# Expert 3's first late gate page: from two row blocks over all 128 partitions to two halves of 64 partitions, asked for at one release

## The reference

```python
def expert_block(args):
    xb, e = args
    hb = jax.nn.silu(xb @ w_gate[e]) * (xb @ w_up[e])
    return hb @ w_down[e]
```

## Time and profile before

| | us |
|---|---|
| median of 3 runs | 1267.19 |
| lowest and highest | 1266.06, 1267.52 |
| the profiled execution | 1266.4 |
| its span | 1264.6 |
| PE busy in the span | 1043.2 (82%) |
| DVE busy | 478.1 (38%) |
| ACT busy | 234.7 (19%) |

### The profile page before, as it was taken

How to read it: one execution, slowest core, us unless ns; L and a number is a source line. 1 busy time by engine, 2 the same in 40 slices (tenths; PEclk the granted TensorE clock), 3 DMA queues, 4 the chain that set the end, 5 groups by cost and what they waited for, 6 DMA issues and landing times.

```text
span 1264.6 us, 22376 instructions
## 1 busy us (share of the span) xinstructions
PE 1043.2 (82%) x9529; PEld 712.1 (56%) x9529; DVE 478.1 (38%) x1230; ACT 234.7 (19%) x526; POOL 4.9 (0%) x27
## 2 busy tenths in 40 slices
PE   9999998766766575889999999999977665758576
PEld 7888755434334352548888888876543333425243
DVE  2342543532222222237665556464343222222223
ACT  2221121111111111113433334121111111111111
POOL 1000000000000000000000000000000000000000
PEclk9999998978787887899999999999887878878789
DMA  9888799999999999996676664899999999999997
GB/s 341 238 338 336 249 430 426 426 428 430 428 429 427 429 429 429 428 392 191 191 230 228 225 217 150 338 362 429 425 428 428 429 427 430 428 430 427 429 428 294
DMA packets 98305, 461.49 MB, mean 365 GB/s; under 512 B 17468, under 2 KB 60728, under 8 KB 73400
## 3 DMA queue, kind: packets, MB, share of 16 engines
q1 hardware_dynamic: 97872, 460.34, 90.6%
q10 hardware_dynamic: 360, 0.15, 0.0%
HBM read 459.38 MB, written 1.08 MB: 364 GB/s over the span
## 4 chain that ended last, share of the span: by engine, by line
PE 52%; DMA 44%; ACT 1%; DVE 1%; issue 1%; SPq 1%; POOL 0%; POOLq 0%; DVEq 0%; ACTq 0%
DMA front<-in_expert_w_up 38%; PE pa L1535 10%; PE pa L1829 8%; PE pb L1535 8%; DMA arena<-in_expert_w_down 6%; PE wa L1829 5%; PE acc L1566 4%; PE wb L1859 3%; PE acc L1684 2%; PE pb L1609 1%; PE acc L1869 1%; PE pb L1785 1%; ACT arena L607 1%; PE wa L2124 1%; DMA w_x<-in_odd_out_proj 1%
## 5 line engine op out<-in xcount | busy, mean ns | idle before, releaser
L1829 PE MATMUL pa<-front,arena 128*32 128x256 f32 x1792 | 127.6, 448 | 77.0 <-DMA front<-in_expert_w_up 77.0
L1290 DVE TENSOR_SCALAR lower<-lower 128x128 f32<-128x128 f32 x64 | 14.4, 225 | 419.1 <-ACT lower L607 419.1
L1829 PE MATMUL wa<-front,arena 128*32 128x256 f32 x1232 | 98.0, 484 | 87.5 <-DMA front<-in_expert_w_up 84.0
L1829 PEld LDWEIGHTS pa<-front,arena 128*32 128x32 f32 x1792 | 62.9, 128 | 144.1 <-DMA front<-in_expert_w_up 89.8
L1829 PEld LDWEIGHTS wa<-front,arena 128*32 128x32 f32 x1232 | 46.9, 138 | 141.6 <-DMA front<-in_expert_w_up 94.0
L607 ACT ACTIVATE arena<-wb 32x256 f32<-32x256 f32 (+2 forms) x236 | 88.9, 377 | 103.4 <-PE wb L1859 95.1
L1859 PE MATMUL wb<-w_dn,conv_raw 128*32 128x256 f32 x1472 | 87.9, 379 | 1.0 <-DMA w_dn<-in_expert_w_down 1.0
L1829 PE MATMUL wa<-w_x,arena 128*32 128x256 f32 x896 | 68.3, 470 | 21.5 <-DMA w_x<-in_expert_w_up 21.5
L1535 PE MATMUL pa<-hnT,w_x 128*128 128x256 f32 x384 | 85.1, 380 | 0.0
L1535 PEld LDWEIGHTS pa<-hnT,w_x 128*128 128x128 f32 x384 | 72.5, 190 | 10.0 <-issue 0.3
L1535 PE MATMUL pb<-hnT,w_x 128*128 128x256 f32 x336 | 74.5, 380 | 0.0
(11 more groups left out here) (345 smaller groups left out, 1248.3 us busy)
## 6 DMA issues: line engine op xcount, KB each, us to landing
w_dn<-in_expert_w_down SPq DMA_DIRECT2D x46, 2048.0 KB, 26.4
front<-in_expert_w_gate SPq DMA_DIRECT2D x42, 2048.0 KB, 20.6
front<-in_expert_w_up SPq DMA_DIRECT2D x42, 2048.0 KB, 25.1
w_x<-in_expert_w_gate SPq DMA_DIRECT2D x15, 2048.0 KB, 31.4
w_x<-in_expert_w_up SPq DMA_DIRECT2D x15, 2048.0 KB, 35.8
arena<-in_expert_w_down SPq DMA_DIRECT2D x14, 2048.0 KB, 25.9
w_x<-in_odd_in_proj SPq DMA_DIRECT2D x16, 1024.0 KB, 5.5
front<-in_expert_w_up SPq DMA_DIRECT2D x10, 1024.0 KB, 8.9
```

The source lines that it names most:

```text
L1290: link(v.tensor_scalar(eg, eg, 1.0, None, ALU.add))
L1829: ins = mm(gu[32 * j:32 * j + 32, :, :], xb[:, k, c0:c0 + CAP], w[k][:, :, P * j:P * j + P], start=(k == 0), stop=(k == KC - 1))
```

## The change

One loop in `expert_stream` is rewritten. It runs once per layer. The bytes, their source, their place in `front` and the increments of the semaphore are the same; the cut and the time of the first request are not.

```diff
                 quarter(l, 3, 0, 0, "gu_res")
+                sp_.wait_ge(S["gu_half"], RELEASES * l + 2)
+                w = expert_w_gate[l, 3].rearrange("(p k) f -> p k f", k=KC)
                 for n in range(2):
-                    sp_.wait_ge(S["gu_half"], RELEASES * l + n + 1)
-                    quarter(l, 3, 0, 1, "gu_in0", 2 * n, 2 * n + 2)
+                    rows = slice(64 * n, 64 * n + 64)
+                    sp_.dma_start(late3[rows, 1, 0], w[rows, 4:8, :]).then_inc(S["gu_in0"], 16)
                 sp_.wait_ge(S["gu_half"], RELEASES * l + 3)
                 quarter(l, 3, 1, 1, "gu_in0")
```

## The result

| | before | after |
|---|---|---|
| median of 22 runs, us | 1266.59 | 1268.32 |
| lowest and highest | 1265.69, 1267.60 | 1267.69, 1269.04 |
| span of the profiled execution | 1264.6 | 1266.5 |

The ratio is 1.0014, with a 95% interval of 1.0008 to 1.0019: 1.7 us slower, about 0.9 us per layer. The forecast was 1.5 us slower.

What follows compares the result with a forecast made beforehand. PE was taken to set the pace early in each MoE stage, then the DMA queue; 16x - 8.6 gave +1.5 us on a 1264.6 us span, so 1267.9 profiled and 1268.7 us median, 8-in-10 range 1263.7 to 1271.0.

Steps and rivals of the forecast that it cites:

- The release and SP's issues: Expert 3's late gate page: first half issued 0.44 us later (layer 1: 0.43), second 0.43 later and hidden; up page's delay hidden.
- The packet of a half: Changed page: 8 KB packets to 64 partitions take twice the full-width time, 0.63 to 0.64 us; chance 0.48.
- x: Time one 8 KB packet of a 64-partition transfer holds its engine; taken as 0.63 to 0.64 us, eight packets per engine.
- the fixed 2.6 us around the packets: Start and completion of the changed page's transfer: 5.2 us from issue to landing, of which 2.6 are packets, leaving 2.6.
- the formula: Changed page lands 2.6 + 8x us after its first issue; over both layers the change is 16x - 8.6, +1.5 us.
- Landing to end: From the page to the layer's end: a loss passes in full, a gain up to 2.0 us per layer.
- the head of the backlog: The changed page, first in a queue said to stay filled from about 148 us (837 in layer 1) until the last expert.
- The uncovered 5.2 us of the up page: Up page right after the changed page: lands 5.2 us after issue when uncovered, against 7.4 and 7.2 before.
- narrow place: Where issue time could cap a gain: the up page, 2.0 us free, and expert 6's gate page, 2.9 us free.
- Rival A: Changed page: halves run at full width, x = 0.32 to 0.38, -3.5 to -2.5 us, at best 1263.7 us; chance 0.27.
- Rival B: Changed page: the fresh queue is slow, not the packet size; x = 0.42 to 0.52, -1.9 to -0.3 us; chance 0.13.
- C: Changed page: Rival B's slowness and sharing of half the partitions multiply; x = 0.84, +4.8 us, 1272.0 us; chance 0.12.

Runs made afterwards that it cites:

- e2: The old row blocks of 4 KB over 128 partitions, both behind release 2: the changed kernel's later request alone; 1266.31 us, ratio to before 0.9998.
- e3: Kernel before the change, with eight other 1 MB late pages in halves of 64 neighbouring partitions, four per layer; 1285.62 us, ratio 1.0156.
- e1: The changed kernel without the halves: expert 3's late gate page as one transfer over all 128 partitions, behind release 2; 1266.60 us, ratio to before 1.0003.
- e5: As e3, but the halves of the eight pages are the even and the odd partitions; 1266.96 us, ratio to before 1.0001.
- e9: The changed kernel with its two halves as even and odd partitions instead of 0 to 63 and 64 to 127; 1266.57 us, ratio to before 1.0003.
- e7: Kernel before the change without expert 3's late gate page, 1 MB less per layer; 1267.26 us, ratio 1.0006.
- e10: Kernel before the change without expert 3's late gate page and the up page behind it, 2 MB less per layer; 1267.08 us, ratio 1.0007.
- e11: Kernel before the change without expert 4's last late page, 1 MB less per layer; 1264.05 us, ratio 0.9983.
- e4: Kernel before the change, with e3's eight pages in two row blocks of 4 KB packets over 128 partitions; 1268.48 us, ratio 1.0016.

## Why the prediction came out right, and where its steps did not

*The release and SP's issues.* As predicted: the first half at 146.89 us (PE's start 0.24 earlier), the up page undisturbed. The delay of 0.44 us was contained in the sum as a cost; e2 shows no cost, though up to 0.9 us over both layers can't be excluded.

*The packet of a half.* The forecast was x = 0.63 to 0.64 for double the full-width time. Measured at the place: 0.55 us from 148 to 152 us, but 0.61 from 150 to 154. In the filled queue of e3 it is 0.59 us (112 packets from 160 to 164 us, share 1.03), and 2.4 us a page. So the mechanism is the one named, shown by e1, e5 and e9, and the size was 3 to 15% too high. In the other direction, the fixed 2.6 us around the packets was too small for two transfers: by x = 0.55 the formula gives 2.6 + 4.4 = 7.0 us, and the page took 7.9 us from the first issue. By 154 us the engines had moved 159 packets of 8 KB, 31 more than the page has, so some were at the up page while others still worked at this one; that such unevenness is the missing time wasn't tried. The two errors cancelled in part: the page was complete at the 154.8 us of the forecast by the clock, but PE and the first request were 0.24 us earlier than in the sum, so it came 1.0 us later than before and not 0.7. In layer 1 it took 8.4 us from the first issue against 7.7.

*Landing to end.* This is the step that failed. It said that whatever moves the head of the backlog moves everything behind it, a loss in full and a gain up to 2.0 us per layer. e1 gained two microseconds on the page and e7 and e10 left out one and two pages, for nothing. The uncovered 5.2 us of the up page was right, as e7 has 5.1. What was wrong stands before it: that the queue holds work without a gap from 148 us. The rows that I read for this begin at 174 us; from 152 to 156 us the share of before is 0.92, and in e1, e7 and e10, where less lies ahead, it is 0.87, 0.93 and 0.73 at 242 to 303 GB/s instead of 367. Part of this is idle time and part a low rate while occupied, whose cause stays open. There the gain is used up but for half a microsecond, at expert 4's pages, which the prediction did not list as a narrow place. At expert 6's gate page I had worked out 7.5 us for an uncovered page, and e11 shows 9.3. Losses pass better, but not whole: 1.0 and 1.6 us on the page became 0.9 and 0.7 at expert 6. The forecast of +0.7 and +0.8 per layer met the measured 0.9 per layer by luck in part: the page's delay was set too low and the share of it that passes too high.

*The rivals.* Rival A's premise, halves at full width, is refuted (0.55 against 0.32 to 0.38 us). Its price would have been wrong too: e1 and e9 are real full-width kernels, the page landing at 152.0 and 152.5 us where A said 152.3, and they run level with before and not 3.5 us faster. The 0.18 that I gave to a gain was owed to the failed step. Rival B was partly right in kind: 4 KB packets are slow at this place (0.26 us each) and fast (0.16 us) in the filled queue of e4. In e1, 8 KB pieces there took 0.37 us against 0.32, so size and place both have a part. C, their product, did not occur.

*No better version came out.* e1 and e9 repair the change and tie with before; neither beats it, and e7 and e10 say why: with the bytes ahead of expert 4's pieces left out altogether, the end does not come earlier.

## What to carry to other kernels

A transfer to half the partitions is priced by which ones it takes: 64 neighbours, or 32, run at a little over half the rate (235 and 238 GB/s against 415) and occupy all engines meanwhile, and a second transfer for the other half behind it gives nothing back. Where a cut by partitions is needed, take every second one, or keep all 128. And a queue that looks full is no proof that a gain at its head counts: leave the transfer out altogether, which takes one run, and see whether the end moves before working on its speed.

## What the runs showed of the hardware that was not expected

Every second partition is as good as all: 415 GB/s for pages cut into even and odd halves, against 235 for neighbouring halves.

A queue that has just been empty starts slowly. In e7, the up page issued at 148.95 us had no page ahead of it:

```profile
148.00:152.00 4.00, 4.00 (x64) 2.55 (x60) 3.29 (x13) 0.09 (x1) 0.00 (x0) 1.00 0.52 135
```

Only 8 of the 66 packets of these four microseconds move before 150 us. They hold an engine for 0.516 x 64 / 66 = 0.50 us each, 260 GB/s per full share, where full-width pages in a filled queue move about 425. In e1 it is 0.41 us from 148 to 150 us and 0.35 in the next two. e11's 9.3 us at expert 6 and the low rates of e1, e7 and e10 at expert 4's pages may be the same thing. That stays open, as does the cause: both were measured, neither was tried.
